# mLSTM mixer of a hybrid trunk: sample values turned later, last head in another order, part of its state work inside the down-projection

## What is computed

```
up = h @ w_up;  xm, z = up[..., :2048], up[..., 2048:]
xc = silu(conv(xm));  q, k = xc_h @ w_q, (xc_h @ w_k) * 512**-0.5;  v = xm_h @ w_v      # 4 heads of 512
li, lf = input gate, log_sigmoid(forget gate);  b = cumsum(lf)
s   = (q k^T) * exp(dmat - m_t)                     # dmat = b_t - b_s + li_s, causal
num = w_inter * (q @ C) + s @ v;  nq = w_inter * (q @ n) + sum(s)
h   = num / max(|nq|, exp(-m_t))                    # then a layer norm per head
C_new = g_state * C + sum_s g_tok * k v^T;  n_new = g_state * n + sum_s g_tok * k
out = ((norm(h) * g_head + skip * xc) * sigmoid(z)) @ w_down
```

## Time and profile before

| what | value |
|---|---|
| median of 3 runs | 1922.34 us (1919.23 to 1925.59) |
| the profiled execution's own time | 1925.8 us |
| its span, first to last instruction | 1924.0 us |
| TensorE busy | 1821.0 us, 95% |
| VectorE busy | 1148.3 us, 60% |
| ScalarE busy | 864.4 us, 45% |
| GpSimd busy | 177.9 us, 9% |
| mean granted TensorE clock | 0.977 |

### The profile page before, as it was taken

One profiled execution on the slowest core, in us unless ns is written; L12 is line 12 of the kernel. 1 busy time (PEld: TensorE's weight loads), 2 busy tenths in 40 slices (PEclk: granted clock), 3 DMA queues, 4 the chain that ended last, 5 costly groups with the idle time before them and its releaser, 6 DMA issues.

```text
span 1924.0 us, 34719 instructions
## 1 busy us (share of the span) xinstructions
PE 1821.0 (95%) x13562; PEld 1677.8 (87%) x13562; DVE 1148.3 (60%) x1843; ACT 864.4 (45%) x1454; POOL 177.9 (9%) x121
## 2 busy tenths in 40 slices
PE   5999898899999999999999999999999898999996
PEld 4999754699999988999987799999999653999995
DVE  5886445566655545655566676556886455566553
ACT  2665311255544465554444555444654311355432
POOL 2000113020010001100120010011000132110011
PEclk9999998899999999999999999999999999999998
DMA  4565322445555533555533155554565223555551
GB/s 130 156 166 169 122 82 99 137 146 172 165 163 173 164 123 104 159 167 165 166 113 108 56 156 163 168 167 144 165 175 169 83 88 110 166 159 161 172 164 58
DMA packets 155869, 272.98 MB, mean 142 GB/s; under 512 B 22677, under 2 KB 28258, under 8 KB 155754
## 3 DMA queue, kind: packets, MB, share of 16 engines
q1 hardware_dynamic: 155754, 271.37, 45.2%
HBM read 250.55 MB, written 20.78 MB: 141 GB/s over the span
## 4 chain that ended last, share of the span: by engine, by line
PE 87%; DVE 8%; ACT 3%; issue 1%; SPq 1%; POOL 1%; DMA 0%; POOLq 0%; ACTq 0%; DVEq 0%
PE PS L1595 85%; PE PS L1600 2%; DVE WLO L974 1%; DVE QT L1246 1%; SPq L352 1%; DVE QT L1251 1%; ACT PB L875 1%; DVE C L1208 0%; DVE BST L1185 0%; DVE XGL L993 0%; DVE TMP L1482 0%; POOL SQ L1526 0%; ACT TMP L926 0%; DVE NT L999 0%; DVE NV L1005 0%
## 5 line engine op out<-in xcount | busy, mean ns | idle before, releaser
L974 DVE TENSOR_TENSOR WLO<-RAWT,WHI 128x512 fp32r<-128x512 f32 (+1 forms) x904 | 644.8, 730 | 505.3 <-ACT WHI L620 503.4
L620 ACT ACTIVATE WHI<-RAWT 128x512 fp32r<-128x512 f32 (+1 forms) x904 | 554.2, 626 | 665.5 <-PE PS L1595 664.9
L1595 PE MATMUL PS<-XGH,WHI 128*128 128x288 f32 x1776 | 527.2, 297 | 17.3 <-DVE WLO L974 17.2
L1595 PE MATMUL PS<-HH,WHI 128*128 128x288 f32 (+1 forms) x1792 | 530.0, 296 | 10.5 <-DVE HL L1273 10.5
L1595 PE MATMUL PS<-HH,WLO 128*128 128x288 f32 (+1 forms) x1792 | 530.8, 296 | 0.0
L1595 PE MATMUL PS<-HL,WHI 128*128 128x288 f32 (+1 forms) x1792 | 529.8, 296 | 0.0
L1595 PE MATMUL PS<-XGH,WLO 128*128 128x288 f32 x1776 | 524.7, 295 | 0.0
L1595 PE MATMUL PS<-XGL,WHI 128*128 128x288 f32 x1776 | 523.8, 295 | 0.0
L1595 PEld LDWEIGHTS PS<-XGH,WHI 128*128 128x128 f32 x1776 | 333.4, 188 | 23.2 <-DVE WLO L974 16.1
L1595 PEld LDWEIGHTS PS<-HH,WHI 128*128 128x128 f32 x1792 | 338.3, 189 | 13.7 <-ACT NST L763 13.5
L1595 PEld LDWEIGHTS PS<-HL,WHI 128*128 128x128 f32 x1792 | 338.3, 189 | 0.0
(11 more groups left out here) (331 smaller groups left out, 1482.2 us busy)
## 6 DMA issues: line engine op xcount, KB each, us to landing
RAWT<-in_w_ff_dram SPq DMA_DIRECT2D x256, 512.0 KB, 3.7
RAWT<-in_a_w_up_dram SPq DMA_DIRECT2D x64, 512.0 KB, 3.8
RAWT<-in_a_w_down_dram SPq DMA_DIRECT2D x32, 512.0 KB, 3.7
RAWT<-in_b_w_qkv_dram SPq DMA_DIRECT2D x24, 512.0 KB, 3.8
RAWT<-in_a_w_q_dram SPq DMA_DIRECT2D x16, 512.0 KB, 3.7
RAWT<-in_a_w_k_dram SPq DMA_DIRECT2D x16, 512.0 KB, 3.8
RAWT<-in_a_w_v_dram SPq DMA_DIRECT2D x16, 512.0 KB, 3.9
C<-in_state_mlstm_C_dram SPq DMA_DIRECT2D x8, 1024.0 KB, 5.5
```

The source lines that it names most:

```text
L620: act.activation(hi, raw, ACT.Copy).then_inc(weight_hi, 1)
L974: dve.tensor_tensor(lo, raw, hi, ALU.subtract).then_inc(weight_lo, 1)
L1595: return pe.matmul(out, lhsT, rhs, start=start, stop=stop, **kw)
```

## The change

- A new tile VS holds a copy of the sample values, in CPST's memory; GpSimd makes it once the gate rows are selected (`gsel_done`). `v_tokens(8..11)` read it and stand behind `broadcast(0)`, in banks 0 and 2; ScalarE's copies of them stand behind `decay(0)`. The mask's DMA waits for eight value copies and for VS. `keys(0)` puts its sample part in bank 3.
- The first value product no longer waits for `kg_out` ahead of itself (the wait behind it stays).
- In the last head QC0 goes to bank 1 and no longer waits for `state(2, 2)`; the new states go to banks 6, 3, 2, 6; the order on TensorE is new state 0, sample product and column, new state 1, norm columns, turn, new state 2, turn of NSB, new state 3, turn of NOUT (now bank 7). VectorE does the sample column and spread, the norm columns, the sample's centring, output and remainder, and only then the last head's own outputs and HL. NST gets memory of its own.
- `old_state(3, 0)` and `(3, 2)` move into the down-projection, ahead of its unit 2, and VectorE's updates of C behind its split 5. SP issues down tiles 4 to 7 ahead of the last head's state output.
- In the latent attention, two semaphores on GpSimd become one with two counts (`css_q` and `css_out`); that part is left out below.

```diff
@@ -171,11 +171,12 @@ memory
+VS = at("VS", [P, AB, TS], o_cp)
-NST = at("NST", [32, P], o_tmp)
+NST = at("NST", [32, P], take(512))
@@ -339,6 +340,9 @@ new function
+def new_bank(h, b):
+    return 3 - b % 2 if h < AH - 1 else (6, 3, 2, 6)[b]
@@ -445,7 +449,8 @@ SP
-            sp.wait_ge(vxp_out, 12 * (la + 1))
+            sp.wait_ge(vxp_out, 12 * la + 8)
+            sp.wait_ge(vs_out, la + 1)
@@ -463,12 +468,15 @@ SP, heads
+                if h == AH - 1:
+                    for t in range(4, 8):
+                        down_tile(t)
-            for t in range(4, 16):
+            for t in range(8, 16):
@@ -709,14 +717,15 @@ ScalarE vtok
-            act.activation(dst, PS[:, 4 + x % 4, :], ACT.Copy).then_inc(vxp_out, 1)
+            bank = 4 + x % 4 if x < 8 else 2 * (x % 2)
+            act.activation(dst, PS[:, bank, :], ACT.Copy).then_inc(vxp_out, 1)
-        for x in range(4, 12):
+        for x in range(4, 8):
@@ -731,7 +740,7 @@ ScalarE state
-            act.activation(CPST[:, q % 2, :], PS[:, 3 - q % 2, :], ACT.Copy).then_inc(cp_out, 1)
+            act.activation(CPST[:, q % 2, :], PS[:, new_bank(q // 4 % AH, q % 4), :], ACT.Copy).then_inc(cp_out, 1)
@@ -740,6 +749,8 @@ ScalarE
+        for x in range(8, 12):
+            vtok(x)
@@ -748,19 +759,20 @@ ScalarE, heads
-            act.activation(QCP[:, 0:512], PS[:, 2, :], ACT.Copy, scale=AECOL[:, 12 + h:13 + h]).then_inc(qcp_out, 1)
-            for b in range(3):
+            act.activation(QCP[:, 0:512], PS[:, 2 if h + 1 < AH else 1, :], ACT.Copy,
+                           scale=AECOL[:, 12 + h:13 + h]).then_inc(qcp_out, 1)
+            for b in range(4):
+                if h == AH - 1 and b == 2:
+                    rsqrt(la, 1, svar_out, sy_out)
-                rsqrt(la, 1, svar_out, sy_out)
+                act.wait_ge(smo_out, la + 1)
+                act.activation(HH[:, 0:AB, TP:T], QT[:, :, TP:T], ACT.Copy).then_inc(smh_hi, 1)
+                act.wait_ge(nst_done, la + 1)
+                act.activation(NST[:], PS[0:32, 7, 128:256], ACT.Copy).then_inc(nst_out, 1)
-            state(4 * U + 3)
-        act.wait_ge(smo_out, la + 1)
-        act.activation(HH[:, 0:AB, TP:T], QT[:, :, TP:T], ACT.Copy).then_inc(smh_hi, 1)
-        act.wait_ge(nst_done, la + 1)
-        act.activation(NST[:], PS[0:32, 0, 0:P], ACT.Copy).then_inc(nst_out, 1)
@@ -1142,7 +1154,6 @@ VectorE ahead of the mask
-        dve.wait_ge(vxp_out, 12 * (la + 1))
@@ -1171,8 +1182,8 @@ VectorE keys
-            dve.tensor_scalar(KGH[:, h % 2, :], PS[:, 1 if h else 5, 0:P], DT[:, 415:416], None,
-                              ALU.mult).then_inc(kg_out, 1)
+            dve.tensor_scalar(KGH[:, h % 2, :], PS[:, 1, 0:P] if h else PS[:, 3, 160:288], DT[:, 415:416],
+                              None, ALU.mult).then_inc(kg_out, 1)
@@ -1224,41 +1235,56 @@ VectorE, heads
+        def columns():
+            ...
+        def sample_column():
+            ...
+        def outputs():
+            ...
+        def remainders():
+            ...
         if h + 1 < AH:
             decay(h + 1)
+            columns()
+            sample_column()
             probs(h + 1)
+            outputs()
+            keys(h + 1)
+            remainders()
+            state(h, 0)
+    sample_column()
+    dve.wait_ge(nqs_out, AH * (la + 1))
+    spread([PS[:, 0, :]], NQS[:], AECOL[:, 24:25], 1, svar_out)
+    columns()
+    dve.wait_ge(sy_out, la + 1)
+    centre([PS[:, 0, :]], [NSB[:]], 1, sn_out)
     dve.wait_ge(sxp_done, la + 1)
     ...
-    state(AH - 1, 2)
+    outputs()
+    remainders()
+    def last_state():
+        state(AH - 1, 0)
+        state(AH - 1, 2)
+    return last_state
@@ -1453,11 +1486,12 @@ VectorE, driver
+        tail = []
-            mix = lambda: mlstm_mix(i, la, evac_last)
+            mix = lambda: tail.append(mlstm_mix(i, la, evac_last))
@@ -1468,7 +1502,7 @@ VectorE, driver
-        stream(dve, res, split, mix, None, lambda g, b: residual(res, g), lambda g: norm_lo(nu, g),
+        stream(dve, res, split, mix, lambda: tail and tail[0](), lambda g, b: residual(res, g), lambda g: norm_lo(nu, g),
@@ -1539,6 +1573,9 @@ GpSimd
+            pool.wait_ge(gsel_done, la + 1)
+            pool.tensor_copy(VS[:], VT_[:, :, TP:T]).then_inc(vs_out, 1)
+            pool.wait_ge(vs_out, la + 1)
@@ -1684,8 +1721,10 @@ TensorE v_tokens
-            if x >= 4:
+            if 4 <= x < 8:
+            if x >= 10:
+                pe.wait_ge(vxp_out, 12 * la + x - 1)
@@ -1693,8 +1732,8 @@ TensorE v_tokens
-                        ins = mm(PS[32 * j:32 * j + 32, 4 + x % 4, b * P:(b + 1) * P],
-                                 VT_[:, 4 * (x - 8) + b, TP:T], IDENT[:])
+                        ins = mm(PS[32 * j:32 * j + 32, 2 * (x % 2), b * P:(b + 1) * P],
+                                 VS[:, 4 * (x - 8) + b, :], IDENT[:])
@@ -1724,7 +1763,8 @@ TensorE keys
-                ins = mm(PS[32 * b:32 * b + 32, 1 if h else 5, 0:P], KT[:, 4 * h + b, TP:T], IDENT[:])
+                out = PS[32 * b:32 * b + 32, 1, 0:P] if h else PS[32 * b:32 * b + 32, 3, 160:288]
+                ins = mm(out, KT[:, 4 * h + b, TP:T], IDENT[:])
@@ -1741,10 +1781,10 @@ TensorE ahead of the heads
-        pe.wait_ge(vxp_out, 12 * (la + 1))
+        pe.wait_ge(vxp_out, 12 * la + 8)
+        pe.wait_ge(cvs_out, la + 1)
-        pe.wait_ge(cvs_out, la + 1)
@@ -1756,6 +1796,9 @@ TensorE ahead of the heads
+        pe.wait_ge(vs_out, la + 1)
+        for x in range(8, 12):
+            v_tokens(x)
@@ -1765,8 +1808,6 @@ TensorE, heads
-            else:
-                pe.wait_ge(kg_out, U + 1)
@@ -1777,67 +1818,98 @@ TensorE, heads
+        last = h == AH - 1
         if h:
             pe.wait_ge(cs_out, 2 * U - 1)
             old_state(h - 1, 2)
-        if h + 1 < AH:
+        else:
+            pe.wait_ge(vxp_out, 12 * (la + 1))
+        if not last:
             broadcast(h + 1)
             scores(h + 1)
-        if h:
-            pe.wait_ge(cs_out, 2 * U)
+            if h:
+                pe.wait_ge(cs_out, 2 * U)
         pe.wait_ge(c0_in[h % 2], 16 * (2 * la + h // 2 + 1))
         for b in range(4):
-            ins = mm(PS[32 * b:32 * b + 32, 2, :], ...)
+            ins = mm(PS[32 * b:32 * b + 32, 1 if last else 2, :], ...)
         ...
         def new_state(b):
             kb = slice(b * P, (b + 1) * P)
-            mm(PS[:, 3 - b % 2, :], KG[:, 0, kb], VTOK[:, 0, vh], True, False)
-            mm(PS[:, 3 - b % 2, :], KG[:, 1, kb], VTOK[:, 1, vh], False, True).then_inc(cp_done, 1)
+            mm(PS[:, new_bank(h, b), :], KG[:, 0, kb], VTOK[:, 0, vh], True, False)
+            mm(PS[:, new_bank(h, b), :], KG[:, 1, kb], VTOK[:, 1, vh], False, True).then_inc(cp_done, 1)
         ...
         new_state(0)
         pe.wait_ge(hvar_out, U + 1)
+        if not last:
+            ...
+            pe.wait_ge(cp_out, 4 * U + 4)
+            old_state(h, 0)
+    sample()
+    sample_column()
+    pe.wait_ge(cs_out, 2 * U)
+    new_state(1)
+    pe.wait_ge(nqs_out, U + 1)
+    columns()
+    turn()
+    new_state(2)
+    pe.wait_ge(sn_out, la + 1)
+    for a in range(4):
+        ins = xp(PS[:, 1, a * P:(a + 1) * P], NSB[:, a * P:(a + 1) * P])
+    ins.then_inc(sxp_done, 1)
+    pe.wait_ge(cp_out, 4 * U + 1)
+    new_state(3)
+    pe.wait_ge(n_out, U + 1)
+    xp(PS[0:32, 7, 128:256], NOUT[:].rearrange("p s f -> p (s f)")).then_inc(nst_done, 1)
+    def last_state():
+        pe.wait_ge(cp_out, 4 * U + 4)
+        pe.wait_ge(nst_out, la + 1)
+        pe.wait_ge(hg_out, U + 1)
+        old_state(AH - 1, 0)
+        old_state(AH - 1, 2)
+    pe.wait_ge(cp_out, 4 * U + 3)
+    return last_state
-    pe.wait_ge(nst_out, la + 1)
-    pe.wait_ge(smo_out, la + 1)
@@ -2152,11 +2224,13 @@ TensorE, driver
-            mlstm_mix(i, la)
+            last_state = mlstm_mix(i, la)
+                if k == 2:
+                    last_state()
```

More of the change, by code:

```diff
@@ L1242, in mlstm_mix @@
[L1242 to L1249, removed]
@@ L1794, in new_state, with columns @@
                         kb = slice(b * P, (b + 1) * P)
-                        mm(PS[:, 3 - b % 2, :], KG[:, 0, kb], VTOK[:, 0, vh], True, False)
-                        mm(PS[:, 3 - b % 2, :], KG[:, 1, kb], VTOK[:, 1, vh], False, True).then_inc(cp_done, 1)
+                        mm(PS[:, new_bank(h, b), :], KG[:, 0, kb], VTOK[:, 0, vh], True, False)
+                        mm(PS[:, new_bank(h, b), :], KG[:, 1, kb], VTOK[:, 1, vh], False, True).then_inc(cp_done, 1)
+                    def columns():
+                        for b in range(4):
+                            kb = slice(b * P, (b + 1) * P)
+                            mm(PS[:, 7, 8 + b:9 + b], KG[:, 0, kb], ONES[:, 0:1], True, False)
+                            mm(PS[:, 7, 8 + b:9 + b], KG[:, 1, kb], ONES[:, 0:1], False, True)
+                        mm(PS[:, 7, 12:16], KGH[:, h % 2, :], HB4[:]).then_inc(n_done, 1)
@@ new lines, in mlstm_mix, with sample, sample_column @@
```

(63 more changed lines are left out.)

75 lines of the change are left out of this document (32 added, 43 removed).

## The result

The changed kernel takes 1872.82 us (median of four, 1868.09 to 1873.32) against 1920.78 us before (median of four, 1918.52 to 1925.59): ratio 0.9746, 95% interval 0.9730 to 0.9762, so 48.0 us less. The forecast was 1884 with a range of 1876 to 1895, 38.6 us less: the sign was right, the size was not, and the range missed the result by 3 us.

What follows compares the result with a forecast made beforehand. TensorE was taken to bound the kernel (87% of the span), with gains only in the two mLSTM mixers. Terms gave 20.0 and 18.6, together 38.6 us, off the median 1922.34: 1883.7, rounded 1884, range 1876 to 1895.

Steps and rivals of the forecast that it cites:

- What follows in heads 0 to 2 is bound by TensorE or by unchanged hand-offs: Heads between front and last head: no gain of their own; the front's shift of 6.9 and 6.0 us carries through.
- 1.64 us between heads: TensorE's gaps at head boundaries, followed by low clock in four of six cases; used to price the down-projection's clock.
- Front, the order: Ahead of the first head: sample values moved behind the broadcast, first value product at 235.2 instead of 239.10, 3.9 us saved.
- rival A: Clock stays low at the first value product and down-projection start: up to 8.0 us lost, 1887 to 1892; chance 0.2.
- GpSimd's copy: Copy of the sample values in the front: 1.2 us long, slowing VectorE beside it by 0.2 us per mixer.
- The last head: Last head's products to down-projection: new order and banks start the down-projection at 341.6, not 355.28, 13.7 us saved per mixer.
- The moved old states: Four old-state products moved between units 1 and 2 of the down-projection: 2.1 us lost per mixer.
- rival B: Down-projection starves at units 3 to 6: 1 to 4 us lost per mixer, 1886 to 1892; chance 0.15.
- The clock at the down-projection: Low clock at its start shrinks: 3.0 and 2.5 us lost before, 1.3 charged after, gain 1.7 and 1.2 us.
- case C: Low stretches at four head boundaries, about 1.7 us each, and ahead of the down-projection vanish too: 1875 to 1878; chance 0.07.

Runs made afterwards that it cites:

- the order undone: The changed kernel with ScalarE copying the fourth new state of heads 0 to 2 behind the HH copy again: 1883.47 us, ratio to before 0.9811.
- the front alone: The kernel before with only VS and its copy, the `v_tokens` order, the earlier mask, bank 3 and no early `kg_out` wait: 1910.46 us, ratio 0.9952.
- the last head alone: The changed kernel with the front as before and ScalarE's old order in heads 0 to 2, moved old states kept: 1893.14 us, ratio to before 0.9860.

## Why the forecast was wrong, point by point

- **The step that failed** is "What follows in heads 0 to 2 is bound by TensorE or by unchanged hand-offs". A hand-off was changed, ScalarE's, and its wait stood in my own text: the "1.64 us between heads" I used only to price the clock. I had read the boundary's rows and its releaser, `CPST`, but followed the diff engine by engine for the last head alone. The runs showed in its place six stops of TensorE, 1.64 us each, that fall away with ScalarE's order: worth 10.7 us of median on the kernel before, and 10.7 to 12.3 us undone in the changed kernel. Without this edit the forecast's 1883.7 met a measured 1883.47, and that is luck in part: the forecast is 38.6 us below 1922.34, the run 35.6 us below a kernel before of 1919.12, and errors of the other terms cancelled as well.
- **Front, the order.** Right in all steps up to the broadcast: gate columns at 229.13 (forecast 229.15), MASKM at 230.19 (230.3), decay tile at 231.10 (231.2), sample values from 230.91 (230.8). But they ended at 236.2, not 235.2, in the first mixer:

```profile
222.55 0.61 POOL L1577 COPY VS<-VT__97 128x512 f32<-128x512 f32 x1 [186.02 <-PE PS L1632]
...
229.13 0.22 PE L1637 MATMUL PS<-IDENT,ROWS 4*128 4x4 f32 x1 [0.63 <-DVE D L1151]
...
230.91 5.37 PE L1632 MATMUL PS<-IDENT,VS 128*32 128x128 f32 x128
...
236.21 2.84 PE L1632 MATMUL PS<-VTOK,PT__101 128*128 128x512 f32 x6
```

  The granted clock was low (1.2 GHz) from 231.4 to 234.8, behind the stop of 0.63 us and the small column products. It was rival A, at the values instead of at the value product, in one mixer of two. In the five profiles with this stop a low stretch follows it in 7 of 10 fronts; with `v_tokens(8)` in the stop's place, in none of 4. The product itself ran at the full clock (236.21 to 239.92 = 3.7 us, forecast 3.65), as forecast.
- **GpSimd's copy.** Forecast 1.2 us long and 0.2 us of delay to VectorE; it took 0.61 us, one row operation grew from 0.30 to 0.33, and the gate rows came at 229.08 against 229.09. Nothing. The Trainium skill's rule on the shared interfaces (GPSIMD Engine Reference, Specifications) did not come into play here: the copy ended at 223.16, and VectorE's next operation with two inputs from memory began at 223.35.
- **The last head.** 13.2 us for 13.7. VectorE took up the sample column 7.3 us behind the products' end (315.80-308.51), forecast 6.3, since its spread and centring of the head were late (rows of before: the earlier trace rows):

```profile
310.75 1.27 POOL L1595 TENSOR_TENSOR KT<-HH,HL 128x512 f32<-128x512 f32 x1
310.89 1.14 DVE L1202 TENSOR_TENSOR LNS<-LNS 128x2 f32<-128x2 f32 x1
...
313.42 1.02 PE L1632 MATMUL PS<-VREP,PT__101 128*32 128x512 f32 x2 [0.84 <-ACT QCP L762]
...
315.80 0.17 DVE L1250 COPY NQS<-PS 32x1 f32<-32x1 f32 x1
...
320.23 0.81 DVE L1210 TENSOR_SCALAR NSB<-PS,MV,LNS 128x512 f32<-128x512 f32 x1
...
322.34 0.69 DVE L1294 TENSOR_TENSOR QT<-PS,COLS 128x512 f32<-128x512 f32 x1 [1.30 <-PE PS L1637]
...
326.11 0.37 PE L1632 MATMUL PS<-HH,WHI 128*128 128x288 f32 x1 [1.98 <-issue]
```

  An operation on two numbers per partition took 1.14 us instead of 0.16, beside GpSimd's KT, and TensorE waited 0.84 us for QCP, not 0.3. From there the steps kept their distances: counted from the products' end, NSB was done at 12.5 us (forecast 11.7), the sample's output began at 13.8 (13.0), the down-projection at 17.6 (17.1).
- **The moved old states.** Mis-sized: 1.07 us each instead of 2.09. The starvation of rival B did not come: no unit waited for WLO.
- **The clock at the down-projection.** A low stretch (327.0 to 330.3) in one mixer of two, which cost 1.5 us (67.2 against 65.7); I had charged 1.3 in each. Right in size.
- **The range.** It was built from the unknown prices and not from a change in a place that I had closed; case C, "the low stretches at the head boundaries fall away too", had the right place but neither its cause nor the stops themselves.

## What to carry to other kernels

Take every changed line through all iterations in which it runs, before sorting it into a part of the change: a loop bound in an engine's order acts on each head. And take every wait that the trace shows on the bounding engine, with its releaser, and ask of each whether the diff touches the releaser's queue; here six waits of 1.64 us had theirs named in the row. A duration for a moved piece of work has to come from a row at the clock at which it will run.

## What the runs showed of the hardware

- A VectorE operation can be held until GpSimd's operation ends. A small one (128x2, two inputs from memory) took 1.14 us beside the start of a GpSimd operation with two inputs, 0.16 us otherwise, and ended with it (310.89+1.14 = 312.03, GpSimd's KT 310.75+1.27 = 312.02). The kernel before has one in its second mixer, 0.74 us long, and it ends 0.02 us behind GpSimd's next operation:

```profile
1610.71 1.05 POOL L1561 TENSOR_TENSOR KT<-KT,COLS 128x512 f32<-128x512 f32 x1
...
1611.04 0.74 DVE L1190 TENSOR_TENSOR LNS<-MV,LNS 128x2 f32<-128x2 f32 x1
```

  The large HL took 1.66 us instead of 1.22 where GpSimd's SX ended 0.57 us after its start. The other way round, SX took 3.32 us instead of 2.37 where VectorE's two-input operation on QT had begun 0.11 us before it (288.73 and 288.84). So the loss was about what was left of the operation that came first, and it weighs most on the shortest operations. The Trainium skill (GPSIMD Engine Reference, Specifications) names two SBUF inputs of VectorE as a case of contention, and a 2-port perf mode as the other: the trace agrees with the first. The operation on the mask (1.69 and 2.01 us instead of 0.38) has one input tile; in which mode it ran no row shows.
- Short stops of TensorE were followed by a stretch at 1.2 GHz in some cases and not in others. In the four profiles that have the six stops of 1.64 us (the kernel before, the order undone, the front alone, the last head alone), a low stretch follows 12 of 24. The stop of 1.98 us ahead of the down-projection was followed by one in 4 of 8 cases, in the changed kernel's profile in one mixer and not in the other.
- Part of the spread between executions goes with the granted clock. The changed kernel's profiled execution had a span of 1866.3 us at 0.991, two others 1871.5 us at 0.988: 0.003 of the mean is (at half rate, twice 0.003 of 1871.5) 11 us more at 1.2 GHz, and half of that, 5.6 us, is lost, against 5.2 us measured. It is not all of it: the fourth execution took 1870.6 us at 0.990, 4.3 us more than the first, where the same estimate gives 1.9.
